# Finer pieces, three state tiles and one modulation part moved: the first block of a two-block kernel on one core

## What is computed

```python
shift_a, scale_a, gate_a, shift_f, scale_f, gate_f = split(silu(c) @ w_ada + b_ada, 6)   # parts 0..5, 1024 wide each
h = layer_norm(x) * (1 + scale_a) + shift_a
q, k, v, z, a, b, gl_q, gl_k, gl_v, gl_g, gl_r = split(h @ w_in)
qkv = silu(causal_dwconv(concat(q, k, v), dn_conv))          # 12 chunks of 128 columns
o_dn = gated_delta_rule(l2_norm(q), l2_norm(k), v, log_a, beta)
o_dn = rms_norm(o_dn, dn_norm_g) * silu(z)

def gla_step(S, inp):                                        # chunks of 64 tokens, 16 of them
    qd_i, kd_i, v_i, oi_i, gl_i = inp
    o = einsum('bhcd,bhde->bhce', qd_i, S) + oi_i
    S = S * gl_i[..., :, None] + einsum('bhcd,bhce->bhde', kd_i, v_i)
    return S, o
o_gla = rms_norm(gla(gl_q, gl_k, gl_v, log_alpha), gla_norm_g) * silu(gl_g)
x = layer_norm(ALPHA * x + gate_a * (concat(o_dn, o_gla) @ w_o))
x = layer_norm(ALPHA * x + gate_f * conv_ffn(x * (1 + scale_f) + shift_f))
```

## Time and profile before

| what | value |
| --- | --- |
| median of 3 runs | 3037.67 us (3035.82 to 3041.81) |
| the profiled execution | 3035.15 us, its span 3033.6 us |
| granted TensorE clock, mean | 0.979 |
| busy: PE, PE weight loads | 2859.8 us, 2236.1 us |
| busy: DVE, ACT, POOL | 1612.7 us, 1013.5 us, 790.8 us |
| instructions | 33367 |

### The profile page before, as it was taken

The page is one execution under the profiler, slowest core; times in us unless marked ns, Lnnn a source line. Parts: engine busy times, 40 slices in busy tenths (PEclk is TensorE's granted clock), DMA queues, the critical chain, the costliest instruction groups (busy, mean ns, idle before and its releaser), DMA issues.

```text
span 3033.6 us, 33367 instructions
## 1 busy us (share of the span) xinstructions
PE 2859.8 (94%) x13340; PEld 2236.1 (74%) x13340; DVE 1612.7 (53%) x2537; ACT 1013.5 (33%) x1575; POOL 790.8 (26%) x456
## 2 busy tenths in 40 slices
PE   6998888999979999999999999999989999999998
PEld 3676556776647888888886778788757888888886
DVE  7545655553575555455557565776444333333335
ACT  2446532233212222222224750565454212222112
POOL 2322112221224444444451113311011222222221
PEclk9999999999999999999999999999999999999999
DMA  7211012222321211111112112013211111111111
GB/s 256 82 33 29 7 56 77 77 84 96 120 83 49 76 49 49 49 49 49 49 49 97 62 50 86 16 31 120 89 36 42 56 49 49 49 49 49 49 49 56
DMA packets 199768, 193.60 MB, mean 64 GB/s; under 512 B 16167, under 2 KB 147647, under 8 KB 199615
## 3 DMA queue, kind: packets, MB, share of 16 engines
q1 hardware_dynamic: 197984, 187.09, 19.5%
q10 hardware_dynamic: 1631, 4.40, 0.4%
HBM read 175.43 MB, written 13.89 MB: 62 GB/s over the span
## 4 chain that ended last, share of the span: by engine, by line
PE 77%; DVE 10%; ACT 7%; issue 3%; POOL 1%; DMA 1%; ACTq 0%; DVEq 0%; SPq 0%; POOLq 0%
PE bank L1315 62%; PE bank L1660 2%; PE bank L1422 1%; PE bank L1463 1%; PE bank L1644 1%; PE bank L1477 1%; PE bank L1612 1%; PE bank L1308 1%; DVE ffn_conv L2308 1%; PE bank L1428 1%; DVE ffn_conv L2304 1%; PE bank L1631 1%; PE bank L1679 0%; PE bank L1408 0%; POOL panel_lo L3065 0%
## 5 line engine op out<-in xcount | busy, mean ns | idle before, releaser
L1315 PE MATMUL bank<-ft_hi,panel_lo 128*128 128x512 f32 x1312 | 467.4, 391 | 1.7 <-DVE ftx_lo L1958 1.7
L3065 POOL TENSOR_TENSOR panel_lo<-panel,panelm_hi 128x1024 fp32r<-128x1024 f32 x64 | 153.3, 2396 | 577.0 <-ACT panelm_hi L2623 531.6
L1315 PEld LDWEIGHTS bank<-ft_hi,panel_lo 128*128 128x128 f32 x1312 | 247.0, 188 | 54.1 <-issue 2.8
L1315 PE MATMUL bank<-ft_hi,panel_hi 128*128 128x512 f32 x704 | 274.0, 389 | 0.0
L1315 PE MATMUL bank<-ft_lo,panel_hi 128*128 128x512 f32 x704 | 273.9, 389 | 0.0
L2304 DVE TENSOR_SCALAR ffn_conv<-ffn_in,ffn_taps 128x512 f32<-128x512 f32 x88 | 114.1, 1296 | 278.8 <-ACT ffn_in L2894 278.7
L2574 DVE TENSOR_TENSOR resid<-resid,bank 128x512 f32<-128x512 f32 x256 | 174.7, 687 | 151.5 <-PE bank L1315 150.7
L3065 POOL TENSOR_TENSOR panel_lo<-panel,panel_hi 128x1024 fp32r<-128x1024 f32 x66 | 157.9, 2401 | 244.3 <-ACT panel_hi L2623 231.1
L1315 PE MATMUL bank<-ft,panel 128*128 128x512 f32 x416 | 197.2, 613 | 7.4 <-ACT v_feat L2771 3.4
L1315 PE MATMUL bank<-ftm_hi,panelm_hi 128*128 128x512 f32 x512 | 200.6, 392 | 2.4 <-DVE ftm_lo L1958 2.4
L1315 PE MATMUL bank<-ftm_lo,panelm_hi 128*128 128x512 f32 x512 | 200.2, 391 | 0.0
(11 more groups left out here) (497 smaller groups left out, 6124.7 us busy)
## 6 DMA issues: line engine op xcount, KB each, us to landing
panel<-in_w_in SPq DMA_DIRECT2D x52, 512.0 KB, 3.9
panel<-in_w_ada SPq DMA_DIRECT2D x48, 512.0 KB, 3.8
panel<-in_ffn_w_up SPq DMA_DIRECT2D x44, 512.0 KB, 3.7
panel<-in_w_mlp_in SPq DMA_DIRECT2D x32, 512.0 KB, 3.9
panel<-in_w_mlp_out SPq DMA_DIRECT2D x32, 512.0 KB, 3.6
panel<-in_w_o SPq DMA_DIRECT2D x24, 512.0 KB, 3.6
panel<-in_w_out SPq DMA_DIRECT2D x24, 512.0 KB, 3.5
panel<-in_ffn_w_down SPq DMA_DIRECT2D x22, 512.0 KB, 3.6
```

What stands on the lines that cost most here:

```text
L1315: m = te.matmul(ps, a, b, start=(start and j == 0), stop=(stop and j == len(pairs) - 1))
L3065: pool.tensor_tensor(lo, k.view(p), hi.bitcast(F32), ALU.subtract).then_inc(*g.new("halved_lo", p))
```

## The change

- **State tiles.** `st_g` becomes three tiles. DVE's update is now `gla_state(n, c)`, which reads tile (2n+c) mod 3 and writes the next one. The update of the first half of a tile moves from the unit state0 to the end of the following prep, two units ahead of the PE step that reads it; the update of the second half moves from state1 to state0. Neither waits any longer for PE's reading of the same step. The last update (second half of tile 7), which nothing reads, and its two matmuls are gone. POOL clears three tiles, and waits for `gla_sum` first, since two of them lie where `keep` and `w_g2` lay.
- **Length sums.** `length` is called for each half: at 8c+10 and 8c+14 in place of both at 8c+13; `unit_length` goes from 8c+15 to 8c+16.
- **Pieces.** z and gg pieces take one 128-row step in place of two: 96 pieces in place of 48, the same matmuls.
- **Away.** A step with no work stands ahead of the delta norm: 168 steps in place of 160.
- **GT_F.** The part leaves `LATE_PARTS`; its eight panels are multiplied on PE by `ada_steps` after the w_o product, ahead of the turning of tiles 6 and 7, with a tile `mod_last` for the banks' contents. `norm_rows` waits for SC_F in its stead.
- **Rows.** The row products of tiles 4 and 5 go from number 6 of the third group to the end of number 7, behind moments, deviation and norm of tiles 6 and 7.

```diff
-LATE_PARTS = (GT_A, SH_F, SC_F, GT_F)
+LATE_PARTS = (GT_A, SH_F, SC_F)
...
-               ["carry", "solve", "out", "norm"])
+               ["carry", "solve", "out", "away", "norm"])
...
+    size = 2 if stage == "qkv" else 1
     for h in halves:
-        for q in range(4):
-            def mult(h=h, q=q):
+        for k0 in range(0, KD, size):
+            def mult(h=h, k0=k0):
...
-    def sums():
-        for h in range(HALVES):
-            k.banks.take(("length", c, h), (0, 1, 2, 3))
-        k.unit("length", c)
-
-    return [(6, sums), (8, lambda: k.unit("unit_length", c))]
+    def sums(h):
+        k.banks.take(("length", c, h), (0, 1, 2, 3))
+        k.unit("length", c, h)
+
+    return [(3, lambda: sums(0)), (7, lambda: sums(1)), (9, lambda: k.unit("unit_length", c))]
...
+    last = [step for steps in spaced(ada_steps(k, GT_F, (2, 3))) for step in steps]
...
-        (2, 4): f2[0:1], (2, 5): f2[1:2], (2, 6): [*f2[2:4], *rows((4, 5))],
-        (2, 7): [lambda: norm_start(k, 1, (6, 7)), *a3]}, split=True, made=made, plain=(1, 2))
+        (2, 4): f2[0:1], (2, 5): f2[1:2], (2, 6): f2[2:4],
+        (2, 7): [lambda: norm_start(k, 1, (6, 7)), *a3, *rows((4, 5))]}, split=True, made=made, plain=(1, 2))
...
     k.unit("ffn_edges")
+    for step in last:
+        step()
     first = [up_panel(0, g) for g in range(2)]
...
+    k.st_g = [place("st_g0", [P, H4, P])] + [place(f"st_g{n + 1}", [P, H4, P], at=top_keep + 4 * BANK * n) for n in range(2)]
...
-                m = te.matmul(ps[:, h * P + c * GC:h * P + (c + 1) * GC], k.st_g[:, h, :],
+                m = te.matmul(ps[:, h * P + c * GC:h * P + (c + 1) * GC], k.st_g[(2 * n + c) % 3][:, h, :],
...
+    def gla_state(n, c):
+        old, new = k.st_g[(2 * n + c) % 3], k.st_g[(2 * n + c + 1) % 3]
+        v.wait_ge(*v.filled("gla", n, f"add{c}"))
+        if n == 0 and c == 0:
+            v.wait_ge("gla_zero")
+        elif c == 0:
+            v.wait_ge("gla_pe", n - 1, "first")
+            v.wait_ge(*v.evicted("gla", n - 1, "add1"))
+        else:
+            if n:
+                v.wait_ge(*v.filled("gla", n - 1, "o"))
+            v.wait_ge(*v.evicted("gla", n, "add0"))
+        ps = v.bank("gla", n, f"add{c}")
+        for h in range(4):
+            rows = slice((h % 2) * GLA_K, (h % 2 + 1) * GLA_K)
+            m = dve.scalar_tensor_tensor(new[rows, h, :], old[rows, h, :], k.g_last[rows, n % 2, h // 2, c:c + 1],
+                                         ps[rows, tile(h)], ALU.mult, ALU.add)
+        evict(m, "gla", n, f"add{c}")
...
             dve.tensor_tensor(k.kd[:], k.kd[:], k.g_qk[:, 2:4, tile(n)], ALU.mult).then_inc(*v.new("gla_dve", n, "k_dec"))
+            if n:
+                gla_state(n - 1, 0)
+        elif s == "state0":
+            if n == NT - 1:
+                gla_state(n, 0)
+            else:
+                gla_state(n, 1)
...
     def gla_start():
-        pool.memset(k.st_g[:], 0.0)
+        g.wait_ge("gla_sum", 1)
+        for st in k.st_g:
+            pool.memset(st[:], 0.0)
...
-                sp.wait_ge(*sp.filled("ada_col", GT_F, 1))
+                sp.wait_ge(*sp.filled("ada_col", SC_F, 1))
```

More of the change, by code:

```diff
@@ L1506, in delta, with length @@
             fill(te.matmul(ps[:], k.ones[:], words(t.sq), start=True, stop=True), "delta", n, "rms")
-    def length(c):
-        for h in range(HALVES):
-            pe.wait_ge("length_squares", c, h)
-            ps = free("length", c, h)
-            fill(te.matmul(ps[:], k.ones[:], k.length[:, half(h)], start=True, stop=True), "length", c, h)
+    def length(c, h):
+        pe.wait_ge("length_squares", c, h)
+        ps = free("length", c, h)
+        fill(te.matmul(ps[:], k.ones[:], k.length[:, half(h)], start=True, stop=True), "length", c, h)
     def gla_gates(h):
```

56 lines of the change are left out of this document (23 added, 33 removed).

## The result

The change makes the kernel slower by 0.43%: 3049.92 us median (3048.25 to 3051.3) against 3035.82 (3034.49 to 3041.81) of the kernel before in the same comparison, ratio 1.0043 (95% interval 1.0032 to 1.0054). The forecast was 3005. The profiled execution of after took 3049.92 us, its span is 3048.7. The experiments ran on several chips, so their ratios, each against runs of before on the same chip, are what is compared.

A forecast was written before the change was run, and what follows sets the result against it. PE in its written order was taken to set the time, with 77% of the chain of waits. Gains of 20 + 0.5 + 12 + 0 = 32.5 us gave 3002.7, as a median 3005 us, range 2985 to 3030.

The forecast's parts named there:

- the paragraph on pieces, away and GT_F's sums: Delta stretch, 425 to 740: 12 us gained, bounds 0 and 22; away's share 4.5, bounds 3 and 5.5.
- 20 were to be gained: GLA stretch, 180 to 360: idle time down 14 us plus 6 us of clock, bounds 5 and 36.
- The forecast's own term: Length sums and masked scores in the GLA stretch: new PE waits of 14 us in all, bounds 0 and 30.
- The chain of 9.1 us: From PE's length sums to POOL's squares: 9.1 us against 7.4 available, a 1.7 us wait in each of seven chunks.
- My second rival: First half's length sum waits for the longest chain every chunk; GLA stretch 19 us longer, kernel at 3045; chance 0.06.
- the length chain: GLA stretch: late next once the state waits fall from 14.5 us to 1.
- 4 us together with DVE's relief: Delta stretch: finer z and gg pieces and DVE's lost multiply-adds gain 4 us, bounds 10 gained and 5 lost.
- the forecast was 0: GT_F on PE and later rows, behind w_o: 0 gained, bounds 3 gained and 8 lost; DVE's gain goes to the panel.
- the 2 us and its part of 4: Delta stretch: 2 us from two big sums PE loses; 4 us for DVE's relief with the finer pieces.
- the clock to fall in long waits only: GLA stretch: with long waits replaced by shorter ones, 6 of the clock's 14.4 us come back.
- my rivals: Whole kernel: engine chain binds, 3025 (0.22); length sums wait, 3045 (0.06); nearly all waits go, 2982 (0.12); GT_F misfits, 3013 (0.08).
- The rule on table loads: ACT in the GLA stretch: the page's table-switch cost would add some 19 us, giving 3024; left out of the forecast.

The follow-up runs named there:

- h1: e9 with one swap: the length root and product issued behind the next chunk's convolution and silu in the same slot; 3013.84 us, ratio 0.9914.
- e9: The change without the step away, second length sum back at delay 6 and root at 8, first sum still early at 3; 3000.20 us, ratio 0.9870.
- e1: The changed kernel with the empty step away taken out again, all else kept; 3022.42 us, ratio 0.9958.
- e3: The changed kernel without the step away and with the old length sums, all other parts kept; 3005.01 us, ratio 0.9896.
- b5: The kernel before with only the three state tiles, earlier updates and dropped last update; 3026.20 us, ratio 0.9965.
- e10: The change without the step away, first length sum back at delay 6, second at 7, root and product at 9; 3018.72 us, ratio 0.9936.
- g2: e9 with ACT's length root at delay 9 and DVE's product at 10, sums still at 3 and 6; 3049.09 us, ratio 1.0036.
- h2: The change without away, length sums at 6 and 7, root at 9, as in e10, but DVE's product at 10; 3014.96 us, ratio 0.9923.
- b6: The kernel before with only GT_F made on PE and the later row products of tiles 4 and 5; 3029.06 us, ratio 0.9971.
- e4: The whole change with only ACT's square of the delta norm moved back, into the step away; 3050.27 us, ratio 1.0044.
- e2: The changed kernel with both length sums at 8c+13 and unit_length at 8c+15 again, away kept; 3038.84 us, ratio 1.0008.
- b3: The kernel before with only the length sums by halves (8c+10, 8c+14, unit_length at 8c+16); 3046.53 us, ratio 1.0035.
- e5: e3 with DVE's delta norm product alone moved one step later; 2998.58 us, ratio 0.9870.

## Why the prediction was wrong

**What failed: away, in the paragraph on pieces, away and GT_F's sums.** It said that one step of delay is over 1 us, longer than the longest wait, and took 4.5 us back. That looks at PE's order alone. The step norm issues three instructions on ACT and one on DVE besides PE's sum, and all of them were moved past what stands in the next slot: on ACT the exponentials of a later tile, which wait for DVE; on DVE the eviction that PE's next left product reads. Neither queue was named. Measured in place of 4.5 gained: 27.5 lost in the change (3049.92 - 3022.42), and 25.5 alone by a median of two groups, 18 to 35. The bounds of 3 and 5.5 had excluded a loss without a reason.

**What failed second: the length sums.** The paragraph saw the very swap that h1 makes, "ACT's silu of chunk c+1 now stands ahead of the logarithm", and booked it as a shorter chain between root and squares. But what the silu waits for, and what stands behind the root on ACT, was not asked. The silu waits for DVE's convolution, and the GLA norm's square stands behind the root. The price shows best against e9, which has the early first sum too but the root at 8. With the root at 9 and the second sum at 7 (e1) PE's waits for the square go from 3.5 to 11.8 us and all four kinds from 21.0 to 32.0; the clock from 180 to 360 falls from 0.97 to 0.91, 0.06 x 180 = 11 us, and the delta scores come 21.5 us later. Against both edits undone (e3) the four kinds are 9.2 us more, 3.0 of them for the square, for which PE waits 8.8 us there as in b5, and the scores come 15 us later, where with the state tiles 20 were to be gained. The forecast's own term was short as well: sums and scores wait 19.3 us, not 14. The chain of 9.1 us behind it was read from rows in which POOL's square was released by ACT's silu; in after DVE's product releases it in all seven chunks:

```profile
POOL length L3189 <- DVE mixed L2225: 84.1, 7, 16.2
```

My second rival put the danger into the single tile: in the change that costs 4 us (3022.42 against 3018.72, e1 and e10), and 34 only when the product comes one delay later still (g2 against h2).

**State tiles: right in mechanism, short by what is late next.** The waits fell from 14.5 to 0.9 us. I named the length chain as late next; it was the GLA norm's square. In b5 its waits are 8.8 us, where the kernel before had only 0.8 for the same square, with 10.0 at the length sums (before 10.5); the gain of the part is 10.1 us.

**Pieces: mis-sized.** I took 4 us together with DVE's relief, bounds 5 lost and 10 gained. Alone the finer pieces gain 13.9 us, all of it in the delta stretch (414.0 for 427.4 us), above the upper bound. My reading is that filler in pieces half as large lets PE come back to a ready step sooner, and that the waits shown were no measure of it; no run here tests this reading by itself. PE's idle time from 425 to 740 goes from 31.6 to 24.6 us and the clock from 0.96 to 0.98:

```profile
425.00:740.00 315.00, 290.41 (x1819) 220.52 (x1820) 170.35 (x317) 96.55 (x182) 66.62 (x48) 0.98 0.26 79
```

**GT_F and the rows: right at the end, mis-sized in the delta stretch.** Behind w_o the forecast was 0, and the rows of after show the mechanism as it was worked out, to be laid beside the earlier trace rows:

```profile
891.05 3.60 PE L1324 MATMUL bank<-panel,g_v 128*128 128x512 f32 x8
...
894.58 2.77 PE L1289 MATMUL bank<-panel,cond 128*32 128x512 f32 x20
...
898.46 1.05 PE L1289 MATMUL bank<-panel,cond 128*32 128x512 f32 x4 [1.11 <-DMA panel<-in_w_ada]
...
901.34 1.54 DVE L1927 TENSOR_SCALAR xhat<-resid,moments,rstd 128x1024 f32<-128x1024 f32 x2
...
906.52 2.95 ACT L2640 ACTIVATE panel_hi<-panel 128x1024 fp32r<-128x1024 f32 x3 [1.87 <-DVE resid L1942]
...
910.08 0.50 PE L1324 MATMUL bank<-ft_hi,panel_hi 128*128 128x512 f32 x1
```

From w_o's second group to the first feed-forward matmul it is 910.08 - 866.64 = 43.4 us, before 896.47 - 852.25 = 44.2. The product fits into the gap, and DVE's gain is given back to the panel, whose splitting waits for the row products. In the delta stretch the relief of DVE was worth more than the 2 us and its part of 4: b6 has 415.4 us there for 427.4, of which the median keeps 8.0.

**The clock.** I expected the clock to fall in long waits only. The worst wait of after from 425 to 740 is 3.8 us, its idle time is nearly that of before (32.9 and 31.6), and the clock is 0.93. One such wait, the 3.55 us that end at 532.19, seen in stretches of after:

```profile
528.00:532.00 4.00, 0.64 (x2) 0.00 (x0) 2.04 (x5) 1.90 (x6) 0.00 (x0) 1.00 0.49 133
532.00:538.00 6.00, 5.81 (x15) 3.75 (x16) 1.03 (x3) 4.02 (x5) 0.00 (x0) 0.51 0.00 0
...
540.00:542.00 2.00, 2.00 (x21) 2.00 (x20) 1.88 (x4) 0.68 (x2) 0.00 (x0) 1.00 0.00 0
```

While PE is idle the clock still reads 1.00. It falls to the lower level, 1.2 GHz, as the work starts again, and PE does the next 6 us at that. e1, without these waits (2.2 us at L1515 are left):

```profile
425.00:740.00 315.00, 291.96 (x1831) 222.46 (x1830) 159.69 (x303) 98.27 (x185) 64.88 (x48) 0.98 0.22 66
```

Of away's loss in this window 32.9 - 23.0 = 9.9 us are idle time and, by an estimate from two rounded means, 0.05 x 315 = 16 the slower clock. e4 against e1 shows it more sharply: only 25.8 - 23.0 = 2.8 us more of idle time, but a clock of 0.92, 19 us.

**The numbers.** The terms that should have stood there: state 10, pieces 14, GT_F and rows 8, away 27 lost, sums 17 lost, the last with the state tiles in place and without away (e1 against e3, 3022.42 - 3005.01). That is 12 lost, 14 were measured. That 3005.0 is both the forecast and what e3 measures is partly chance: against before e3 is 21.6 us shorter in the delta stretch, where 12 were forecast, and 9.4 ahead of it, where it was 20.5. Of my rivals none had a loss in the delta stretch.

**The rule on table loads.** The rule weighed in the prediction (the Trainium skill, ScalarE: Activation LUTs, What ACT_TABLE_LOAD costs: a drain of about 1380 ns besides the load) is not borne out here: in e9 the logarithm starts 0.01 us behind the load's end (218.66 + 1.28 = 219.94, start 219.95), the copy ahead of that load ends 0.02 us before it (218.64 and 218.66), and the second load follows in the same way. Nor did the later root add switches. ACT's loads from 180 to 410 are 53 in after and 54 before, and 58 in e9, which is further on in the program at 410. The chain got late by its place, not by its length.

## What to carry to other kernels

A step that is moved by one place is moved on every engine that has a share in it: write down, for each queue, which instruction it changes places with, whom that one waits for, and what stands behind. A chain that others wait for (square, logarithm, exponential on ACT) should stand ahead of an instruction that must wait for another engine, so that the chain fills the wait; a delay belongs on the instruction that consumes a result, not on the chain that makes it, unless that instruction also frees what another engine waits for (the length product in g2). Where a change of several parts gives nothing, take out the parts that only reorder first: here two of six cost 45 us, and the rest gained 31. The rule on the chain rests on two places of one kernel.

## What the runs showed of the hardware

How much short waits can cost by the granted clock: behind 3.55 us of idle time TensorE ran at 0.51 of 2.4 GHz from 532 to 538 (after), and two matmuls took 2.08 us where they take 1.12 at full clock. In the window of 315 us the clock's part of the loss was larger than the idle time that went with it, by the estimates above 16 to 9.9 us (after against e1) and 19 to 2.8 (e4 against e1); likewise 25 to 10.9 for e2 against e3 (idle 29.2 and 18.3 us, clock 0.91 and 0.99).

The sum of idle time does not tell the clock: after has 32.9 us at 0.93, b3 32.7 at 0.97, e4 25.8 at 0.92, e9 17.4 at 1.00, e5 10.7 at 0.99. Nor does the length of one wait alone: 2.49 us in e4 (up to 537.17) were followed by eight small matmuls of 1.94 us for 1.00, 2.35 us in after (up to 492.50) by two large ones at full clock, 1.13 us. What decides between them no run here shows.

Each ACT table load took 1.28 us with no gap behind it, so the root of one chunk costs ACT 5.0 us, of which 2.6 are loads.
